# SwiGLU gate and up products streamed in two halves of 256 columns

## The chip, the cores and the metric

The kernel runs on one NeuronCore of a Trainium2 chip. The metric is the device time of one execution in microseconds (us). Three runs of the kernel before took 2365.91, 2370.27 and 2372.9 us; their median is 2370.27.

## The reference

A decoder trunk of two layers over 512 positions with a model width of 1024. Each layer computes a half-step of a gated feed-forward network (FFN), a mixer of three kinds of attention heads, a second FFN half-step, and a gated per-layer embedding. The part that the change touches is the FFN, with an inner width of 2816; it occurs twice in each layer, four times in all:

```python
def swiglu(h, w_gate, w_up, w_down):
    return (jax.nn.silu(h @ w_gate) * (h @ w_up)) @ w_down

for i in range(DEPTH):                       # DEPTH = 2
    x = x + 0.5 * swiglu(rms_norm(x, ffn1_norm[i]), ffn1_w_gate[i], ffn1_w_up[i], ffn1_w_down[i])
    x = x + hybrid_mixer(rms_norm(x, mix_norm[i]), ...)
    x = x + 0.5 * swiglu(rms_norm(x, ffn2_norm[i]), ffn2_w_gate[i], ffn2_w_up[i], ffn2_w_down[i])
    ...
```

All inputs are float32. `h @ w_gate` is 512 x 1024 by 1024 x 2816.

## The kernel before

**Layout.** The residual stream x is kept transposed in on-chip memory: 8 tiles of 128 features by 512 positions (KT = 8, P = 128, SEQ = 512). A product puts a weight block of 128 x 128 into TensorE as the stationary operand and streams the 512 positions of one tile of x past it, so an output is 128 output features by 512 positions in one bank of the accumulation memory (2 KB per partition, 512 float32). The norm is applied afterwards: a product is scaled by a factor per position (tile rb).

**Precision.** Every weight and every activation is split in two float32r parts, a rounded one and the rest (wh and wl, xh and xl). A product of one block is three matmuls, made by `three` (lines 502 to 505): wh with xh, wh with xl, and wl with xh, all accumulated in the same bank. Line 503 is the first, 504 the second, 505 the third. Each matmul of the language makes two records in the profile, a weight load (PEld, LDWEIGHTS) and a matmul (PE, MATMUL).

**FFN on TensorE.** `ffn` (line 541) runs over FT = 22 tiles of the inner width. For each tile `ft` it makes the gate product and then the up product with `from_x` (line 512): it takes the next of four banks, waits until the chunk's split weights are there, runs over the 8 blocks k with three matmuls each, 24 in all, and lets the last matmul increase the semaphore "product". The gate product of `ft` 0 waits before each block for the x tile that it needs; in the second FFN it takes the blocks in another order. After the up product of `ft` 0 comes the sum of squares for the norm (`sum_squares`, line 531). After all 22 tiles the down products follow (ffh and ffl are the streamed operands there).

**The other engines in an FFN.** The weights come in chunks of 512 KB, one per product, into three slots of raw, wh and wl. SyncE's queue (line 430) issues a chunk's transfer when the split of the chunk three before is complete. ScalarE rounds raw to wh (line 955) once the product that used the slot is done; VectorE subtracts to get wl (line 1425). For each tile VectorE scales the gate product (line 1512) when its "product" semaphore has come, ScalarE takes the SiLU (line 1019), VectorE scales the up product (line 1525), multiplies (line 1530) and subtracts (line 1518), and ScalarE rounds the result to ffh (line 1024). The order on each engine is written out by hand; engines meet only at semaphores.

**Other stages that the prediction reads.** In the mixer's group C four chunks of "natural" products stream 402 columns of weights past blocks of xh and xl, with the same `three`. `compressed_scores` (line 759) makes products of 128-column weights with 64 streamed columns in plain float32, `transposes` (line 801) turns 128 x 128 blocks.

Of the kernel before, what the change touches and what calls it, by code (L numbers as in the profile page):

```python
# [41 lines left out]
P = 128  # L42
D_MODEL, SEQ, DEPTH, PLE_DIM, D_FF = 1024, 512, 2, 256, 2816
# [11 lines left out]
KT = D_MODEL // P  # L55
# [115 lines left out]
def chunk_width(key):  # L171
    if key[0].startswith("nat"):
        return 2 * NAT[key[0][3]]
    if key[0].endswith("_down"):
        a, b = THIRDS[key[2]]
        return (b - a) * P
    if key[0] == "wout_early":
        return len(LOADED) * P
    if key[0] == "wout_late":
        return 2 * len(LATE) * P  # L180
    return WIDE
# [15 lines left out]
class Counts:  # L197
# [13 lines left out]
    def tick(self, kind, *key, frees=None, layer=None):  # L211

        key = (self.layer if layer is None else layer, *key)
        self.n[kind] = self.n.get(kind, 0) + 1
        assert (kind, *key) not in self.seen, (kind, *key)
        self.seen[(kind, *key)] = self.n[kind]
        if frees is not None:
            content = (self.layer, frees)
            assert content not in self.frees, content
            self.frees[content] = (kind, *key)  # L220
        return self.sem(kind), 1

    def done(self, kind, *key, layer=None):

        if not self.known:
            return self.sem(kind), 1
        return self.sem(kind), self.known["seen"][(kind, self.layer if layer is None else layer, *key)]

    def freed(self, content, layer=None):

        if not self.known:
            return self.sem("any"), 1
        kind, layer, *key = self.known["frees"][(self.layer if layer is None else layer, content)]
        return self.done(kind, *key, layer=layer)
# [6 lines left out]
def layers(nc, a, known):  # L241
# [3 lines left out]
    with ctx:  # L245
# [6 lines left out]
        def sb(name, shape, dt=F32):  # L252
            size = int(np.prod(shape[1:])) * 4
            t = nc.alloc_sbuf_tensor_at(name, shape, dt, offset=place["at"])
            place["at"] += (size + 63) // 64 * 64
            assert place["at"] <= 229344, (name, place["at"])
            return t

        x = sb("x_res", [P, KT, SEQ])
        xh, xl = sb("xh", [P, KT, SEQ], F32R), sb("xl", [P, KT, SEQ], F32R)  # L260
# [121 lines left out]
        tick, done, freed = counts.tick, counts.done, counts.freed  # L382
# [26 lines left out]
        with nc.Block() as block:  # L409
# [74 lines left out]
            def _(pe):  # L484
                turn, held = {0: 0, 1: 0, 2: 0}, {}

                def take(content, which=1, at=None):

                    if which == 2:
                        which, at = SHARED[turn[2] % len(SHARED)]  # L490
                        turn[2] += 1
                    elif at is None:
                        at = turn[which] % 4
                        turn[which] += 1
                    if (which, at) in held:
                        layer, old = held[which, at]
                        pe.wait_ge(*freed(old, layer=layer))
                    held[which, at] = (counts.layer, content)
                    counts.bank[(counts.layer, content)] = (which, at)
                    return (main, side)[which][at]  # L500

                def three(out, lh, ll, rh, rl, start, stop, **kw):
                    nc.tensor.matmul(out, lh, rh, start=start, stop=False, **kw)  # L503
                    nc.tensor.matmul(out, lh, rl, start=False, stop=False, **kw)  # L504
                    return nc.tensor.matmul(out, ll, rh, start=False, stop=stop, **kw)  # L505

                def chunk(key):
                    c, n = counts.layer * NCHUNKS + CHUNK[key], chunk_width(key)
                    pe.wait_ge(*done("weights_lo", c, layer="all"))
                    return wh[:, c % SLOTS, 0:n], wl[:, c % SLOTS, 0:n]  # L510

                def from_x(key, stage=None, at=None, order=tuple(range(KT)), read=False):

                    out = take(key, 0, at)
                    h, l = chunk(key)
                    for k in order:
                        if stage:
                            pe.wait_ge(*done("x_lo", stage, k))
                        ks = slice(k * P, (k + 1) * P)
                        mm = three(out[:], h[:, ks], l[:, ks], xh[:, k, :], xl[:, k, :], k == order[0],  # L520
                                   k == order[-1])
                        if read and k < KT - 1:
                            mm.then_inc(*tick("x_read", k))
                    mm.then_inc(*tick("product", key))

                def sum_squares(name):

                    out = take(("squares", name))
                    pe.wait_ge(const_in, 16)
                    pe.wait_ge(*done("squares_added", name, KT - 1))  # L530
                    nc.tensor.matmul(out[:], const_("ones"), acc[:], start=True,
                                     stop=True).then_inc(*tick("squares", name))

                def head_squares(name, blocks, n=SEQ, which=1):
# [3 lines left out]
                    nc.tensor.matmul(out[:, 0:n], const_(blocks), zs[:, slot_of(name) % 2, 0:n], start=True,  # L538
                                     stop=True).then_inc(*tick("head_squares", name))

                def ffn(name):
                    for ft in range(FT):
                        if ft:
                            from_x((name + "_gate", ft))
                        else:
                            from_x((name + "_gate", ft), name,
                                   order=EARLY + LATE if name == "ffn2" else tuple(range(KT)))
                        from_x((name + "_up", ft))
                        if ft == 0:
                            sum_squares(name)  # L550
                    for dt in range(KT):
                        out = take((name + "_down", dt), 0)
                        for third, (lo, hi) in enumerate(THIRDS):
                            key = (name + "_down", dt, third)
                            h, l = chunk(key)
                            for f in range(lo, hi):
                                if dt == 0:
                                    pe.wait_ge(*done("h_lo", name, f))
                                fs = slice((f - lo) * P, (f - lo + 1) * P)
                                mm = three(out[:], h[:, fs], l[:, fs], ffh[:, f, :], ffl[:, f, :], f == 0,  # L560
                                           f == FT - 1)
                            if third < 2:
                                mm.then_inc(*tick("product", key))

                        mm.then_inc(*tick("product", key))
# [343 lines left out]
                for layer in range(DEPTH):  # L909
                    counts.layer = layer  # L910
                    ffn("ffn1")
                    group_c()
                    hgrn()
                    attention()
                    products_out()
                    ffn("ffn2")
                    for h2 in range(2):
                        key = ("ple_proj", h2)
                        h, l = chunk(key)
                        pe.wait_ge(*done("emb_lo", 1))  # L920
                        for d in range(4):
                            out = take(("ple_out", 4 * h2 + d), 0)
                            for k in range(2):
                                ks = slice((2 * d + k) * P, (2 * d + k + 1) * P)
                                mm = three(out[:], h[:, ks], l[:, ks], embh[:, k, :], embl[:, k, :], k == 0, k == 1)
                            mm.then_inc(*(tick("product", key) if d == 3 else tick("product", key, d)))
                        if h2 == 0:
                            sum_squares("ple")
                    for dt in range(KT):
                        from_x(("ple_gate", dt), "ple" if dt == 0 else None, read=dt == KT - 1 and layer < DEPTH - 1)  # L930
                        if dt == 0:
                            sum_squares("post")
# [1210 lines left out]
```

## Time and profile before

| | |
|---|---|
| median of 3 runs | 2370.27 us |
| profiled execution | 2371.97 us |
| its span (first to last instruction) | 2370.2 us |
| mean granted TensorE clock | 0.984 |
| instructions recorded | 27606 |
| TensorE matmul busy | 2286.1 us, 96%, 10816 matmuls |
| TensorE weight load busy | 1803.5 us, 76%, 10816 loads |
| VectorE busy | 1208.1 us, 51% |
| ScalarE busy | 901.6 us, 38% |

Busy time is the time in which at least one instruction of that kind is in flight. Matmuls are pipelined: one starts before the one ahead has left the array, so the duration of a single matmul is longer than the step from one start to the next, and the step is what a row of matmuls costs. Weight loads run beside matmuls and have rows of their own. The granted clock is given as a share of 2.4 GHz.

### The profile page before, as it was taken

To read this page: it belongs to the slowest core of one execution; us is meant where nothing else is said; L and a number is where in the kernel's file an instruction comes from. 1 tells how busy PE (TensorE), PEld (TensorE's weight loads), DVE (VectorE), ACT (ScalarE), POOL (GpSimd) and SP (SyncE) were. 2 spreads that over 40 slices of the span, in tenths; PEclk is the share of its full clock that TensorE was granted. 3 is DMA by queue.
4 is the path that set the end of the run, shared out by engine and by line. 5 is a ranking of instruction groups with operands and counts; after the bars stand their busy time and mean duration, and the time that the engine had idled before them with its cause. 6 is when DMAs were issued, how large, how long until landed. Compare 5 with 4: busy or idle time off the path is not lost. (4 is left out here: it accounts for less than half of the span.)

```text
span 2370.2 us, 27606 instructions
## 1 busy us (share of the span) xinstructions
PE 2286.1 (96%) x10816; PEld 1803.5 (76%) x10816; DVE 1208.1 (51%) x1990; ACT 901.6 (38%) x1483; POOL 82.6 (3%) x119
## 2 busy tenths in 40 slices
PE   8999999899989999999999999998989889999998
PEld 6888887776656788888778888877766568888887
DVE  5444334465676444433564443345657764444335
ACT  5222223444654323222453232244445643232224
POOL 0000000032000000000000000001310000000000
PEclk9999999999989999999999999999999899999999
DMA  5333334211102233333233333343121023333332
GB/s 193 121 98 98 91 96 150 94 54 63 45 21 78 89 98 93 99 99 102 89 98 90 98 95 98 99 132 102 55 72 34 21 80 98 98 95 99 98 101 80
DMA packets 68986, 214.31 MB, mean 90 GB/s; under 512 B 8143, under 2 KB 15311, under 8 KB 68858
## 3 DMA queue, kind: packets, MB, share of 16 engines
q1 hardware_dynamic: 59344, 189.27, 26.2%
q10 hardware_dynamic: 9514, 23.27, 2.9%
q8 instruction: 87, 1.43, 0.2%
q14 instruction: 41, 0.34, 0.0%
HBM read 208.30 MB, written 5.40 MB: 90 GB/s over the span
## 5 line engine op out<-in xcount | busy, mean ns | idle before, releaser
L503 PE MATMUL main<-xh,wh 128*128 128x512 f32 x1944 | 778.0, 400 | 16.4 <-DVE xl L1432 12.5
L504 PE MATMUL main<-xl,wh 128*128 128x512 f32 x1944 | 761.9, 392 | 0.0
L505 PE MATMUL main<-xh,wl 128*128 128x512 f32 x1944 | 761.5, 392 | 0.0
L1425 DVE TENSOR_TENSOR wl<-raw,wh 128x1024 fp32r<-128x1024 f32 (+3 forms) x372 | 440.1, 1184 | 399.9 <-ACT wh L955 399.0
L955 ACT ACTIVATE wh<-raw 128x1024 fp32r<-128x1024 f32 (+3 forms) x372 | 378.2, 1017 | 498.2 <-PE main L505 466.6
L503 PEld LDWEIGHTS main<-xh,wh 128*128 128x128 f32 x1944 | 367.6, 189 | 121.8 <-issue 21.2
L505 PEld LDWEIGHTS main<-xh,wl 128*128 128x128 f32 x1944 | 367.9, 189 | 78.1
L504 PEld LDWEIGHTS main<-xl,wh 128*128 128x128 f32 x1944 | 368.0, 189 | 77.9 <-issue 4.3
L503 PE MATMUL main<-ffh,wh 128*128 128x512 f32 x704 | 273.9, 389 | 0.0
L504 PE MATMUL main<-ffl,wh 128*128 128x512 f32 x704 | 273.9, 389 | 0.0
L505 PE MATMUL main<-ffh,wl 128*128 128x512 f32 x704 | 273.9, 389 | 0.0
L1019 ACT ACTIVATE fg<-fg 128x512 f32<-128x512 f32 x88 | 55.7, 632 | 403.6 <-DVE fg L1512 403.5
L1512 DVE TENSOR_TENSOR fg<-main,rb 128x512 f32<-128x512 f32 x88 | 60.8, 691 | 240.0 <-PE main L505 225.2
L504 PEld LDWEIGHTS main<-ffl,wh 128*128 128x128 f32 x704 | 132.2, 188 | 27.5
L505 PEld LDWEIGHTS main<-ffh,wl 128*128 128x128 f32 x704 | 132.2, 188 | 27.4
L503 PEld LDWEIGHTS main<-ffh,wh 128*128 128x128 f32 x704 | 132.2, 188 | 27.4
L1525 DVE TENSOR_TENSOR fu<-main,rb 128x512 f32<-128x512 f32 x88 | 60.8, 691 | 156.4 <-PE main L505 156.4
L1300 ACT ACTIVATE probs<-probs,small 128x128 f32<-128x128 f32 (+3 forms) x160 | 87.7, 551 | 38.5 <-DVE small L1827 38.5
L476 POOL TENSOR_TENSOR zv<-ev,hall 128x256 f32<-128x256 f32 x108 | 80.4, 767 | 317.0 <-ACT ev L1117 218.4
L1668 DVE COPY_PREDICATED sdiag<-lmask,side 128x512 f32<-128x512 uint32 x84 | 57.1, 733 | 42.5 <-PE side L621 42.5
L621 PEld LDWEIGHTS side<-zv 64*128 64x128 f32 x768 | 48.1, 187 | 29.1 <-issue 24.7
L621 PE MATMUL side<-zv 64*128 64x128 f32 (+1 forms) x768 | 59.4, 292 | 8.0 <-DVE cp L1788 5.2
(230 smaller groups left out, 1937.7 us busy)
## 6 DMA issues: line engine op xcount, KB each, us to landing
raw<-in_ffn_gate SPq DMA_DIRECT2D x88, 512.0 KB, 3.6
raw<-in_ffn_up SPq DMA_DIRECT2D x88, 512.0 KB, 3.6
raw<-in_ffn_down SPq DMA_DIRECT2D x64, 448.0 KB, 3.3
raw<-in_w_in_t SPq DMA_DIRECT2D x40, 512.0 KB, 3.6
raw<-in_ffn_down SPq DMA_DIRECT2D x32, 512.0 KB, 3.5
raw<-in_wout SPq DMA_DIRECT2D x24, 384.0 KB, 3.1
w<-in_cmp_w ACTq DMA_DIRECT2D x16, 512.0 KB, 3.6
raw<-in_ple_gate SPq DMA_DIRECT2D x16, 512.0 KB, 3.2
```

Of the source, the lines that this page charges most:

```text
L476: nc.gpsimd.tensor_tensor(o.rearrange(cut, two=2, l=size)[:, :, which, :], e.rearrange(cut, two=2, l=size)[:, :, which, :], operand.rearra ...
L503: nc.tensor.matmul(out, lh, rh, start=start, stop=False, **kw)
L504: nc.tensor.matmul(out, lh, rl, start=False, stop=False, **kw)
L505: return nc.tensor.matmul(out, ll, rh, start=False, stop=stop, **kw)
L621: mm = nc.tensor.matmul(outs[hh][:, o:o + w], first[:, s:s + P], second[:, t:t + w], start=True, stop=True)
L955: nc.scalar.activation(wh[:, c % SLOTS, 0:n], raw[:, c % SLOTS, 0:n], ACT.Copy).then_inc(*tick("weights_hi", c, layer="all"))
L1019: nc.scalar.activation(fg[:, ft % 2, :], fg[:, ft % 2, :], ACT.Silu).then_inc(*tick("gate_silu", name, ft))
L1300: nc.scalar.activation(pr, pr, ACT.Exp, bias=sm("nm", k), scale=-1.0, accum_out=sm("sum", k)).then_inc(*tick("probs", u, g, i))
L1425: nc.vector.tensor_tensor(wl[:, c % SLOTS, 0:n], raw[:, c % SLOTS, 0:n], wh[:, c % SLOTS, 0:n], ALU.subtract).then_inc(*tick("weights_lo", ...
L1512: nc.vector.tensor_tensor(fg[:, ft % 2, :], bank_of((name + "_gate", ft))[:], rb[:], ALU.mult).then_inc(*tick("gate_scaled", name, ft, fre ...
L1525: nc.vector.tensor_tensor(fu[:, ft % 2, :], bank_of((name + "_up", ft))[:], rb[:], ALU.mult).then_inc(*tick("up_scaled", name, ft, frees=( ...
L1668: ins = V.copy_predicated(out, m, src)
```

## The change

A function `in_halves` stands beside `from_x`. For each weight block it runs `three` twice, over positions 0 to 255 and over 256 to 511, into the two halves of the same bank: six matmuls of 256 columns for three of 512. Only the very first matmul of a product has the start flag; both halves of the last block end with the stop flag. The last matmul of all increases the same semaphore as before. `ffn` calls it for every up product and for all gate products but that of `ft` 0. Nothing changes on other engines, in the down products, in the mixer or in the embedding.

```diff
+                def in_halves(key, stage=None):
+
+                    out = take(key, 0)
+                    h, l = chunk(key)
+                    for k in range(KT):
+                        if stage:
+                            pe.wait_ge(*done("x_lo", stage, k))
+                        ks = slice(k * P, (k + 1) * P)
+                        for half in range(2):
+                            ns = slice(half * SEQ // 2, (half + 1) * SEQ // 2)
+                            mm = three(out[:, ns], h[:, ks], l[:, ks], xh[:, k, ns], xl[:, k, ns], k + half == 0,
+                                       k == KT - 1, skip_group_check=True)
+                    mm.then_inc(*tick("product", key))
+
                 def ffn(name):
                     for ft in range(FT):
                         if ft:
-                            from_x((name + "_gate", ft))
+                            in_halves((name + "_gate", ft))
                         else:
                             from_x((name + "_gate", ft), name,
                                    order=EARLY + LATE if name == "ffn2" else tuple(range(KT)))
-                        from_x((name + "_up", ft))
+                        in_halves((name + "_up", ft))
                         if ft == 0:
                             sum_squares(name)
```

## Rows read from the trace of the kernel before

**Rows 1.** Profile page: span, busy time by engine, granted clock in 40 slices.
```profile
span 2370.2 us, 27606 instructions
...
PE 2286.1 (96%) x10816; PEld 1803.5 (76%) x10816; DVE 1208.1 (51%) x1990; ACT 901.6 (38%) x1483; POOL 82.6 (3%) x119
...
PEclk9999999999989999999999999999999899999999
```

**Rows 2.** Windows, FFN stretches: length, busy and count by engine, PEclk, DMA share, GB/s.
```profile
28.00:256.00 228.00, 228.00 (x1007) 188.69 (x1005) 108.30 (x147) 73.60 (x93) 0.00 (x0) 1.00 0.35 111
...
785.00:1012.00 227.00, 227.00 (x1003) 187.94 (x1002) 105.68 (x126) 68.96 (x88) 0.00 (x0) 1.00 0.31 95
1205.00:1434.00 229.00, 229.00 (x1010) 189.26 (x1009) 108.93 (x148) 74.26 (x94) 0.00 (x0) 1.00 0.32 96
1961.00:2187.00 226.00, 226.00 (x999) 187.20 (x998) 104.89 (x125) 67.23 (x86) 0.00 (x0) 1.00 0.31 96
```

**Rows 3.** Groups of instructions, 28.7 to 256 us: count | busy, mean ns | idle before.
```profile
L503 PE MATMUL main<-xh,wh 128*128 128x512 f32 x335 | 130.3, 389 | 0.0
L503 PEld LDWEIGHTS main<-xh,wh 128*128 128x128 f32 x335 | 62.9, 188 | 13.1
...
L955 ACT ACTIVATE wh<-raw 128x1024 fp32r<-128x1024 f32 x41 | 43.1, 1052 | 50.3 <-PE main L505 50.3
L1512 DVE TENSOR_TENSOR fg<-main,rb 128x512 f32<-128x512 f32 x22 | 15.2, 691 | 56.7 <-PE main L505 54.9 <-ACT rb L982 1.9
```

**Rows 4.** Timeline inside gate and up products: start us, duration us, engine, instruction.
```profile
100.28 0.39 PE L503 MATMUL main<-xh,wh 128*128 128x512 f32 x1
100.28 0.19 PEld L504 LDWEIGHTS main<-xl,wh 128*128 128x128 f32 x1
...
103.68 0.39 PE L503 MATMUL main<-xh,wh 128*128 128x512 f32 x1
...
109.12 0.39 PE L503 MATMUL main<-xh,wh 128*128 128x512 f32 x1
```

**Rows 5.** Timeline at the start, the granted clock still at 1.2 GHz.
```profile
16.29 0.63 PE L503 MATMUL main<-xh,wh 128*128 128x512 f32 x1
...
18.42 0.63 PE L505 MATMUL main<-xh,wl 128*128 128x512 f32 x1
```

**Rows 6.** Timeline of the natural products of group C, 402 columns.
```profile
444.18 0.34 PE L505 MATMUL main<-wh,xl 128*128 128x402 f32 x1
...
446.02 0.34 PE L503 MATMUL main<-wh,xh 128*128 128x402 f32 x1
...
444.19 0.19 PEld L503 LDWEIGHTS main<-wh,xh 128*128 128x128 f32 x1
```

**Rows 7.** Timeline of a restart of TensorE at 584.6 us.
```profile
584.61 0.19 PEld L503 LDWEIGHTS main<-xh,wh 128*128 128x128 f32 x1 [0.33 <-issue]
584.61 0.50 PE L503 MATMUL main<-xh,wh 128*128 128x512 f32 x1
...
584.72 0.19 PEld L504 LDWEIGHTS main<-xl,wh 128*128 128x128 f32 x1
```

**Rows 8.** Timeline of dense runs: 24 score products, 11 transposes (merged rows).
```profile
556.09 2.88 PEld L759 LDWEIGHTS side<-kc,q 128*128 128x128 f32 x24
556.32 2.79 PE L759 MATMUL side<-kc,q 128*128 128x64 f32 x24
...
649.42 1.35 PEld L801 LDWEIGHTS side<-const,probs 128*128 128x128 f32 x11
649.65 1.36 PE L801 MATMUL side<-const,probs 128*128 128x128 f32 x11
```

**Rows 9.** Timeline: the two square-sum products in plain float32; one lasts 0.59 us.
```profile
27.29 1.02 PE L531 MATMUL side<-acc,const 128*128 128x512 f32 x2
...
L531 PE MATMUL side<-acc,const x20: 590/590/591, 27.3 to 2326.1; 128*128 128x512 f32 x20
```

**Rows 10.** DMA queues of the page: packets, MB, share of 16 engines' time.
```profile
q8 instruction: 87, 1.43, 0.2%
```

## Prediction, made before the changed kernel was run

> **What bounds the kernel now.** I began with the page. TensorE's matmul row is busy for 2286.1 of 2370.2 us, against 51% for VectorE and 38% for ScalarE, and the granted clock is 9 tenths or more in nearly every slice [rows 1]. Busy time of pipelined matmuls does not say what one costs, so I then read the four stretches in which the changed products run, 910 us in all: matmul is busy in every microsecond of them, at a granted clock of 1.00 (2.4 GHz) [rows 2]. In the groups of instructions of the first stretch the matmuls have 0.0 us of idle before them, while VectorE and ScalarE sit idle waiting for a product (54.9 us in 22 scalings of a gate product, 50.3 us in 41 splits of weights) [rows 3]. So in these stretches TensorE sets the pace and every nanosecond of the start-to-start step of its matmuls is on the path. The timeline gives that step: 24 matmuls between 103.68 and 109.12 us, 5.44 us / 24 = 226.7 ns [rows 4]. The duration shown for one (389 ns) is its latency, and no price for the sum.
>
> **What changes in number.** A gate or up product is now 8 weight blocks x 3 matmuls of 512 columns = 24. Each becomes 48 of 256 columns. The first gate product of each of the four FFN calls keeps its form, so 4 x (21 + 22) = 172 products change: 4128 matmuls and 4128 weight loads go, 8256 of each come. Today every matmul has its own load, also where the next one uses the same weights (as many load as matmul records, 335 and 335 for the same line) [rows 3], so the second half loads all three blocks again. Nothing is saved for that: the columns streamed are the same. With P for the step at 256 columns, the change costs 4128 x (2P - 226.7 ns). It pays off only below P = 113.3 ns.
>
> **What P can be, from below.** Streaming 256 columns at 2.4 GHz takes 106.7 ns. A load also needs time of its own. At a restart the second load starts 0.11 us after the first and the first matmul, recorded as 0.50 us where 0.39 is usual, really starts then too [rows 7]: a load of 128 columns takes some 107 to 110 ns before its matmul can go on. Where the streaming is much shorter than that, the load is the step: the 24 score products with 64 moving columns have 24 loads in 2.88 us; without the last one's duration (0.19) and the longer first gap (0.23), 2.46 / 22 = 111.8 ns [rows 8]. Transposes of 128 columns with 128-column loads go every (1.36 - 0.27) / 10 = 109 ns [rows 8]. So loads hide up to a step of about 112 ns and P is not below 111.8. That end of the range is a gain of 4128 x 3.1 ns = 13 us, with the load in front instead of the stream.
>
> **What P can be, from above.** At 512 columns the step is 226.7 where the columns alone are 213.3: 13.4 ns too many. At the 1.2 GHz level the surplus is gone: 5 matmuls in 2.13 us are 426 ns, the 512 columns alone 426.7 [rows 5]. The question of this change is what the 13.4 ns belong to. If to the columns (6.3% more for each), 256 columns take 113.3 and the change is free. If to the matmul with its load, 256 columns take 106.7 + 13.4 = 120.0, and 4128 x 13.3 = 55 us are added. The one other width of this number format in the trace is 402 columns: 10 steps in 1.84 us, 184.0 ns, 16.5 over its 167.5 [rows 6]. By the proportional reading it should be 178, by the fixed one 180.9; it is above both and nearer the fixed one. Its rows of 402 x 4 bytes start off a power of two, which may cost a little that halves of 256 don't pay. A surplus of 16.5 would give 123.2 and +81 us; a straight line through both widths (0.388 ns a column) 127.3 and +115 us. I take 120.0, as the 512-column row has the tensor and alignment of the changed code.
>
> A rule of the Trainium skill bears on this. The surplus at 2.4 GHz measured above is 13.4 ns; the skill (TensorE: Matmul & The Clock Gate, Back-to-back issue gap) states a gap of N/2.4 + 2.5 ns, for an isolated matmul and not named for this number format. The 4-byte products of the square sums, two 512-column ones in 1.02 us, step by 1.02 - 0.59 = 0.43 us [rows 9], close to twice 213.3, so a small surplus as in that rule does occur in this kernel, but the row of the changed products doesn't follow it. By that rule the change would cost 4128 x 2.5 ns = 10 us.
>
> **What else the edit touches.** The semaphore increment stays on the last matmul of a product, and the wait for weights ahead of the first, so VectorE, ScalarE and the weight queue see the same events, each product at most some 0.3 us later (24 x 13.3 ns). They wait for TensorE today [rows 3], so none of this is late. Cover for nothing is removed: the weight chunks are read in the same order, and a slower product gives their transfer and splits more time. The bank is started once, by the first half of the first block, and costs no instruction. Instruction fetch: 1.43 MB in 87 packets, 0.2% of the DMA engines [rows 10], is 66 bytes for each of the 21632 matmul and load records if it is all theirs. Two records every 120 ns would be 1.1 GB/s beside the 95 to 111 GB/s of these stretches [rows 2]; I cost it at nothing. If it couldn't keep up, TensorE would wait for instructions, which no row of the old kernel excludes at 8256 pairs on end; the longest dense run is about 24 [rows 8]. The clock stays up in either case, since TensorE never rests.
>
> **Sum.** Profiled execution 2371.97 us (span 2370.2 and 1.8 around it) + 55 = 2427; the median of the runs shown is 1.7 lower, so 2425.3, said as 2426.
>
> **Rivals.**
> 1. The surplus belongs to the columns (P 111.8 to 114.5): -13 to +10 us, 2357 to 2380. For it: a read rate that a 2.4 GHz stream just exceeds would give a surplus for each column and none at 1.2 GHz, as [rows 5] have it, and the surplus per matmul of [rows 9] is small. Against: the 184 ns of [rows 6], which this reading puts at 178. This is the case that ends on the other side: if a 256-column stream and a load fit under each other with less loss than a 512-column one, steps below 113.3 make the kernel faster. It decides below 113.3 ns, and the load-bound 111.8 caps the gain at 13 us. Chance 25%: 4 faster by over 0.3% (7.1 us), 15 within, 6 slower (P above 114.2).
> 2. The forecast, P 117 to 124: +30 to +88 us. Chance 45%.
> 3. Loads and streams share something: (512 + 128) / 226.7 = 2.82 columns per ns and (402 + 128) / 184.0 = 2.88 agree within 2%. Then (256 + 128) / 2.85 = 134.7 and +176 us, 2546; with the straight line above this case runs from P 125 to 136. Against it: each half of the agreement rests on one width, and the 402-column rows already carry an alignment of their own. Chance 20%.
> 4. A load must end before the next matmul starts: its record is 188 ns [rows 3], it starts with the matmul before it [rows 4], so P = 188 and 4128 x 149.3 = +616 us, 2986; or instruction supply binds somewhere between. Against: at 402 columns the next matmul starts every 184 ns, before the load's record ends [rows 6], and the dense run with 0.19 us loads goes every 112 ns [rows 8]. Chance 10%, most of it for something smaller than 188.
>    Loads are busy 62.9 x 3 = 189 of 228 us in the first stretch, 83% [rows 2, 3]. By the Trainium skill (Perfetto Trace Analysis, Identifying the Most-Contended Engine) it is the load's busy share, not the matmul's, that tells the headroom; twice the loads would be 166% and it speaks for this rival. But busy loads overlap in [rows 8] (24 x 0.19 us in 2.88 us), so I don't take that share as a bound.
> 5. The change does not do what it says, for instance a second load dropped where weights repeat: today none is dropped, so it is inside the above and has no chance of its own.
>
> **Numbers.** About 0.3% (7.1 us) is what a measurement of this kernel can tell from no change. Faster 4%; same 15%; slower 45 + 6 + 20 + 10 = 81%. The likeliest case's own range is 2400 to 2458. For 8 in 10 I reach down to 2368 (P at 113) and up to 2500 (P at 129), leaving out the gain (3), the upper part of rival 3 (7) and rival 4 (10).
>
> **What the new profile would show.** 14944 matmul and load records in place of 10816; in the gate stretches groups of 128x256 with 2752 records a line (8256 / 3) beside 512-column groups; a product of 48 matmuls taking 48P: 5.44 us if free, 5.76 by my forecast, 6.5 by rival 3, 9.0 by rival 4. The down products' step should stay 226.7 and the rest of the kernel unchanged, granted clock 1.00 in the gate stretches. If loads start evenly spaced and well after the matmul before them, the load is the bound; if they start with it, the stream is. I am wrong in direction if 48 matmuls take less than 5.42 us, and wrong in kind if the extra time stands as idle time ahead of matmuls (engine or instruction waits) and not in their steps.

## The result, and the profile after

The changed kernel takes 2425.76 us (median of 4 runs, 2417.94 to 2427.51), the kernel before 2368.09 on the same chip. The ratio is 1.0237, 95% interval 1.0205 to 1.0268: slower by 2.4%. The forecast was 2426.

The page of the kernel after, to be read against [rows 1]: 8256 records more, 4128 of them matmuls and 4128 loads. TensorE is as busy as before in share of the span and 51.9 us busier; the load row, which is where the doubled loads show, has grown by 213 us. VectorE and ScalarE have the same work.

```profile
span 2423.5 us, 35862 instructions
...
PE 2338.0 (96%) x14944; PEld 2016.7 (83%) x14944; DVE 1208.3 (50%) x1990; ACT 902.4 (37%) x1483; POOL 82.7 (3%) x119
...
PEclk9999999999999999999999999999999899999999
```

The groups of instructions of the first changed stretch (28.7 to 267 us), against [rows 3]. No idle time stands before a matmul; the engines behind it wait longer than before (62.4 us in place of 56.7 ahead of the scaling of the gate products, 56.6 in place of 50.3 ahead of the splits).

```profile
L503 PE MATMUL main<-xh,wh 128*128 128x256 f32 x663 | 187.6, 283 | 0.0
L503 PEld LDWEIGHTS main<-xh,wh 128*128 128x128 f32 x662 | 127.1, 192 | 0.0
...
L969 ACT ACTIVATE wh<-raw 128x1024 fp32r<-128x1024 f32 x41 | 43.2, 1054 | 56.6 <-PE main L505 56.6
L1526 DVE TENSOR_TENSOR fg<-main,rb 128x512 f32<-128x512 f32 x22 | 15.2, 691 | 62.4 <-PE main L505 60.9 <-ACT rb L996 1.5
```

The window of that stretch, against [rows 2]: matmul and load busy throughout, granted clock 1.00.

```profile
28.00:267.00 239.00, 239.00 (x1992) 238.81 (x1991) 107.86 (x148) 73.87 (x94) 0.00 (x0) 1.00 0.34 107
```

The timeline inside the new products, against [rows 4]: a load starts with the matmul ahead of it (both at 100.06 us), and 48 matmuls go from 100.18 to 105.94 us, 5.76 us / 48 = 120.0 ns. Over all 8248 neighbouring pairs of 256 columns the mean without the gaps is 120.00.

```profile
100.06 0.28 PE L505 MATMUL main<-xh,wl 128*128 128x256 f32 x1
100.06 0.19 PEld L503 LDWEIGHTS main<-xh,wh 128*128 128x128 f32 x1
...
100.18 0.28 PE L503 MATMUL main<-xh,wh 128*128 128x256 f32 x1
...
105.94 0.28 PE L503 MATMUL main<-xh,wh 128*128 128x256 f32 x1
```

Where the time went, by stage. The marks are the starts of TensorE's square sums and of the first down product in the traces; us. A gate/up stretch here begins behind the two products of tile 0, so it holds 42 changed products. "Mixer" is everything between the down products of FFN 1 and the square sums of FFN 2.

```
stage            before: layer 0, layer 1    after: layer 0, layer 1
gate/up, FFN 1          229.4   229.4            242.8   242.8
gate/up, FFN 2          229.4   229.4            242.8   242.8
down, each              125.1   125.1            125.1   125.1
mixer                   401.7   398.0            397.6   401.4
```

The first stretch ends with the first down product, at 256.68 us in the kernel before and 270.10 us in the changed one:

```profile
256.68 0.39 PE L503 MATMUL main<-ffh,wh 128*128 128x512 f32 x1
```

```profile
27.30 0.63 PE L531 MATMUL side<-acc,const 128*128 128x512 f32 x1
...
270.10 0.40 PE L503 MATMUL main<-ffh,wh 128*128 128x512 f32 x1
```

Each of the four stretches grew by 13.4 us: 42 x 24 x 13.3 ns. With the four up products of tile 0 that makes 55, and the span grew by 53.3. The rest is the mixer and the start, which move by some us from execution to execution, and so does the time that the granted clock spends at 1.2 GHz. By the profile's record of that clock, which begins 18 to 19 us after the first instruction, it is 74 us before and 67 after.

### The profile page after: what moved, and what is told of

It reads as the page before. It is cut to its first block and busy times, and to the rows that moved or that the text cites. A ratio compares the mean times of both kernels' runs of the same rounds, so it can differ in the third digit from the quotient of the medians.

```text
span 2423.5 us, 35862 instructions
## 1 busy us (share of the span) xinstructions
PE 2338.0 (96%) x14944; PEld 2016.7 (83%) x14944; DVE 1208.3 (50%) x1990; ACT 902.4 (37%) x1483; POOL 82.7 (3%) x119
## 5 line engine op out<-in xcount | busy, mean ns | idle before, releaser
L503 PE MATMUL main<-xh,wh 128*128 128x256 f32 (+1 forms) x3320 | 1021.7, 308 | 16.2 <-DVE xl L1446 12.4
L504 PE MATMUL main<-xl,wh 128*128 128x256 f32 (+1 forms) x3320 | 1005.0, 303 | 0.0
L505 PE MATMUL main<-xh,wl 128*128 128x256 f32 (+1 forms) x3320 | 1005.0, 303 | 0.0
L503 PEld LDWEIGHTS main<-xh,wh 128*128 128x128 f32 x3320 | 630.7, 190 | 67.9 <-issue 21.9
L504 PEld LDWEIGHTS main<-xl,wh 128*128 128x128 f32 x3320 | 631.2, 190 | 24.3 <-issue 4.3
L505 PEld LDWEIGHTS main<-xh,wl 128*128 128x128 f32 x3320 | 630.7, 190 | 24.3
```

## The experiments

The theory of the prediction: a step is the streamed columns at 2.4 GHz plus 13.3 ns, but no less than the 111.8 ns that a 128-column load needs. The rivals are a cost of the stretch as a whole, a cost of the order, and a surplus that hangs on something other than the matmul count. Experiments 3 to 8 ask what the surplus hangs on.

**1. Half of the change.** Only the up products in halves.

```diff
                         if ft:
-                            in_halves((name + "_gate", ft))
+                            from_x((name + "_gate", ft))
```

> Only the up products run in halves, the gate products go back to 512 columns. Theory (each matmul pays a fixed 13.3 ns on top of its columns, whatever its width): 88 products x 24 matmuls x 13.3 ns = 28.2 us over the kernel before, half of the change's 55; step 120.0 ns in the up products, 226.7 in the gate products, ratio 1.012. Rival (the cost is one of the stretch as a whole, such as instruction supply or the weight slots running late): gate products alone give the other engines and the fetch time to catch up, and the cost is well under half.

2397.17 us against 2368.61, ratio 1.0119 (1.0101 to 1.0136): +28.6 us for 28.2. Each of the four stretches takes 236.5 us, within 0.4 us of halfway between 229.4 and 242.8. The cost adds up matmul by matmul; nothing in it points to the other engines or to the supply of instructions, and experiment 8 settles that supply, since there the same number of instructions takes 113.3 ns each.

**2. Another order, twice.** First the halves as the outer loop.

```diff
-                    for k in range(KT):
-                        ks = slice(k * P, (k + 1) * P)
-                        for half in range(2):
-                            ns = slice(half * SEQ // 2, (half + 1) * SEQ // 2)
+                    for half in range(2):
+                        ns = slice(half * SEQ // 2, (half + 1) * SEQ // 2)
+                        for k in range(KT):
+                            ks = slice(k * P, (k + 1) * P)
```

> The loop over the two halves is outside the one over the weight blocks: all 24 matmuls on columns 0 to 255, then 24 on 256 to 511, same number and size. Theory (fixed cost per matmul): step 120.0 ns and the same time as the changed kernel, 2424 to 2427 us. Rival (returning to the same weight block or hopping between the halves of the bank costs or saves something): another step, by more than 1 ns, that is over 8 us in all.

2421.84 us. The four stretches take 242.8 us as in the changed kernel, mean step 119.99 ns; the 4 us less, which also put the time 2 us under the expected range, lie outside them, in an execution with 50 us recorded at the low clock in place of 67. Then equal weights side by side:

```diff
+                        for n, (weights, moving) in enumerate(((h, xh), (h, xl), (l, xh))):
+                            for half in range(2):
+                                ns = slice(half * SEQ // 2, (half + 1) * SEQ // 2)
+                                mm = nc.tensor.matmul(out[:, ns], weights[:, ks], moving[:, k, ns],
...
```

> Halves with the order turned so that equal weights stand next to each other: both halves of wh with xh, both of wh with xl, both of wl with xh; four loads of wh follow each other. Theory (every matmul loads its weights again, whatever was there): 14944 loads, step 120.0 ns, the time of the changed kernel, 2420 to 2427 us. Rival (a repeated load is cheaper or is skipped): fewer load records or a step towards the 113.3 ns at which the change would be free, about 2370 us.

2431.07 us (before: 2371.2 beside it), 4 us over the expected range, with 81 us recorded at the low clock; 14944 loads, mean step 120.00 ns, stretches 242.8 us again. A repeated load is made all the same, and the step does not change. So neither of two other orders rescues the change. Whether a repeated load is a cheaper one can't be seen here, as the step is longer than a load needs.

**3. Narrower pieces: is there a load floor?**

```diff
-                        for half in range(2):
-                            ns = slice(half * SEQ // 2, (half + 1) * SEQ // 2)
+                        for n, (lo, hi) in enumerate(((0, 128), (128, 256), (256, 384), (384, 512))):
+                            ns = slice(lo, hi)
...
```

> The same products cut into four pieces of 128 columns, with four loads a block. Theory with a load floor: the stream would need 66.7 ns, but each 128-column load holds the next matmul until 111.8 ns, so 4 x 111.8 = 447 ns in place of 226.7, 4128 x 220.5 = +910 us, about 3280 us, loads evenly spaced at 112 ns and no longer starting with a matmul. Rival, only the fixed cost of a matmul counts: 4 x 66.7 = 266.7, +165 us, about 2535 us.

3278.12 us, 2 us from the forecast of the floor. Its timeline shows how a load-bound stretch looks: the loads come every 112 ns, in between the matmuls' starts, where in the stream-bound one they start with a matmul. 24 matmuls from 149.86 to 152.54 us are 111.7 ns each. It is one execution, as are those of experiments 4 to 7; they are read by their steps.

```profile
149.86 0.27 PE L503 MATMUL main<-xh,wh 128*128 128x128 f32 x1
149.91 0.19 PEld L504 LDWEIGHTS main<-xl,wh 128*128 128x128 f32 x1
149.97 0.28 PE L504 MATMUL main<-xl,wh 128*128 128x128 f32 x1
150.02 0.19 PEld L505 LDWEIGHTS main<-xh,wl 128*128 128x128 f32 x1
...
152.54 0.27 PE L503 MATMUL main<-xh,wh 128*128 128x128 f32 x1
```

**4. Uneven pieces.** The same edit with `((0, 384), (384, 512))`:

> The same products cut unevenly, 384 + 128 columns. Theory (step = the larger of columns / 2.4 GHz + 13.3 ns and the 111.8 ns that a 128-column load needs): 173.3 for the wide piece, about 112 for the narrow one, pair 285.3 ns in place of 226.7, 4128 x 58.6 = +242 us, about 2610 us. Rival without a load floor: 173.3 + 66.7 = 240.0, the same +55 us as the halves, 2424 us.

2619.91 us: 10 above the forecast, far from the rival's 2424. A block of six takes 150.34 to 151.20 us, 0.863 by all of them where 0.856 was expected. If the three narrow ones take 111.7 each, 176 ns are left for a wide one, 2.6 more than 173.3. And with `((0, 402), (402, 512))`:

> Cut 402 + 110 columns, the wide piece starting at the beginning of its row. It asks what lay behind the 184.0 ns of the 402-column products of the mixer. If their rows, which start off a power of two, were the cause: 167.5 + 13.3 = 180.8 ns here. If 402 columns cost more by their number: 184.0. If the surplus is a share of the columns: 178.0. The 110-column piece is under the load floor: 112 ns in each case. Pair 290 to 296 ns, +261 to +286 us, 2630 to 2655 us.

2656.05 us, 1 above the expected range; the steps inside the 402-column group are 183.3 and 180.8 on average. Starting a row evenly takes only 1 to 3 of the 184.0 ns away. Both runs say that 13.3 ns is not one price for all widths. One more thing stands in this trace: three of its four stretches take 296.5 or 296.6 us, a mean step of 146.67 ns, and FFN 2 of layer 0 takes 299.9 us at 148.33, with the same instructions.

```profile
150.34 0.40 PE L503 MATMUL main<-xh,wh 128*128 128x384 f32 x1
150.57 0.34 PE L504 MATMUL main<-xl,wh 128*128 128x384 f32 x1
150.75 0.34 PE L505 MATMUL main<-xh,wl 128*128 128x384 f32 x1
150.92 0.22 PE L503 MATMUL main<-xh,wh 128*128 128x128 f32 x1
150.98 0.27 PE L504 MATMUL main<-xl,wh 128*128 128x128 f32 x1
151.09 0.28 PE L505 MATMUL main<-xh,wl 128*128 128x128 f32 x1
151.20 0.39 PE L503 MATMUL main<-xh,wh 128*128 128x384 f32 x1
```

**5. Fewer weight columns: what does the surplus hang on?**

```diff
+                    m = 64 if key[1] >= 4 else P
                     for k in range(KT):
...
-                        ks = slice(k * P, (k + 1) * P)
...
+                        ks = slice(k * P, k * P + m)
+                        for n, (lo, hi) in enumerate(((0, 512),)):
...
-                            mm = three(out[:, ns], ...
+                            mm = three(out[0:m, ns], ...
```

The first two runs stream 512 columns in one piece again, the third one four pieces of 128; in each the first four tiles of an FFN keep all 128 weight columns.

> One matmul of 512 columns per block again, but from the fifth tile of each FFN on only 64 of the 128 weight columns are loaded (left out: half the output features of 144 of the 172 products, the bank's other rows keep what was there). It asks what the surplus of 13.3 ns hangs on. If on the loaded columns (the load takes a share of the stream's time, 0.104 ns a column): half, 6.7 ns, step 220.0, 3456 x 6.7 = 23 us under the kernel before, about 2346 us. If it is one of the matmul, whatever is loaded: step 226.7 and the time of the kernel before, 2369 us.

> As the run with 64 weight columns, with 32 (left out: three quarters of the output features of the same 144 products). If the surplus hangs on the loaded columns: 3.3 ns, step 216.7, 35 us under the kernel before, about 2334 us. If it belongs to the matmul: 226.7 again, 2369 us.

Both expectations missed, on the same side. 2381.58 us with 64 weight columns and 2384.13 with 32, against 2367.19, one execution each: a smaller load makes the 512-column matmul slower. 12 steps take 2.76 us in the timeline, 230 ns; with 32 columns the mean is 231.7. The surplus is neither a share of the load nor fixed.

```profile
149.72 0.40 PE L503 MATMUL main<-xh,wh 128*64 128x512 f32 x1
...
152.48 0.40 PE L503 MATMUL main<-xh,wh 128*64 128x512 f32 x1
```

> Four pieces of 128 columns, with 64 weight columns loaded from the fifth tile of each FFN on (left out: half the output features there). The other 28 products are quarters with full loads, 672 x 220.5 = +148 us. For the 144: a load of 64 columns should hold a matmul for about 58 ns only (53 + 4.5), so the stream binds again. Surplus on loaded columns: 53.3 + 6.7 = 60.0 ns, 3456 x (240 - 226.7) = +46, about 2563 us. Surplus of the matmul: 66.7 ns, +138, about 2655 us. If the load floor doesn't shrink with the loaded columns: 111.8 here too, +762, about 3280 us.

2560.37 us, 60.0 ns a step (24 in 1.44 us), 3 us from the forecast for a surplus on the loaded columns. The two runs before had already refuted that one, so its match is no support. What stays is that the floor shrinks with the loaded columns, and that the surplus at 128 streamed columns is 6.7 ns, half of 13.3.

```profile
150.49 0.22 PE L503 MATMUL main<-xh,wh 128*64 128x128 f32 x1
...
151.93 0.22 PE L503 MATMUL main<-xh,wh 128*64 128x128 f32 x1
```

**6. A table of widths.** One kernel in which each tile's products stream one shape over and over.

```diff
+                    if key[1] >= 4:
+                        m, n, at = (GATES if key[0].endswith("gate") else UPS)[key[1] - 4]
                     for k in range(KT):
-                        ks = slice(k * P, (k + 1) * P)
-                        for half in range(2):
-                            ns = slice(half * SEQ // 2, (half + 1) * SEQ // 2)
+                        ks = slice(k * P, k * P + m)
+                        for rep in range(-(-SEQ // n)):
+                            ns = slice(at, at + n)
...
```

> A table of steps in one run. From the fifth tile of each FFN on, each gate product streams one width over and over into the first columns of its bank, as often as it takes to reach 512 columns in all, with 128 weight columns: 128, 160, 192, 224, 240, 256, 272, 288, 320, 352, 384, 402, 416, 432, 448, 480, 496, 512 streamed columns. The up products do so with 64, 32 and 96 weight columns, and with 256 columns that start at 8, 64 and 256 (left out: all columns and features outside these, and columns are added more than once, so the outputs are not the model's). The total time says nothing here, the steps do. Theory 1 (fixed cost of a matmul, 13.3 ns, under a load floor of 111.8): 111.8 up to 224 columns (224 gives 106.7), then columns / 2.4 + 13.3: 113.3 at 240, 120.0 at 256, 146.7 at 320, 180.8 at 402, 200.0 at 448, 226.7 at 512, the same at every start. Theory 2 (after the runs with 64 weight columns, 60.0 ns at 128 columns and 230 at 512): a surplus of about 3.3 ns + 0.026 ns a column, which with 64 weight columns gives 116.7 at 256 and 173.3 at 384, and with 128 weight columns breaks down only because something adds a few ns to the narrow ones. Theory 3: the surplus comes in whole steps, least where the width divides evenly into 256, 13.3 ns there and 15 to 17 in between, as 402 and 384 showed.

The steps, worked out from the starts of each product of 24 to 96 matmuls without its first two, median of four products of a shape; the four agree within 0.04 ns (for 128 weight and 512 streamed columns the step of the unchanged products). In brackets what stands above columns / 2.4 GHz.

```
streamed columns    128 weight columns    96              64             32
128                 111.7  (load floor)   85.0            60.0  (6.7)    60.0  (6.7)
160                 111.7  (load floor)
192                 111.6  (load floor)                   88.7  (8.7)
224                 111.7  (load floor)
240                 112.0
256                 120.0  (13.3)         116.0 (9.3)     113.5 (6.8)    113.3 (6.7)
272                 125.2  (11.9)
288                 131.7  (11.7)
320                 146.6  (13.3)                         144.4 (11.1)
352                 160.0  (13.3)
384                 173.3  (13.3)                         173.3 (13.3)   173.2 (13.2)
402                 183.5  (16.0)
416                 188.2  (14.9)
432                 196.1  (16.1)
448                 202.7  (16.0)                         202.4 (15.8)
480                 216.7  (16.7)
496                 223.3  (16.7)
512                 226.7  (13.3)         229.9 (16.6)    230.1 (16.7)   231.1 (17.8)
```

With 128 weight columns, 256 streamed ones that start at column 64 step by 119.8 ns, at 256 by 120.0, and 384 that start at 128 by 173.9.

None of the three theories holds as written. Theory 1 has the floor up to 224 and, with full loads, the value at 256, 320, 352, 384 and 512, but not at 240 (112.0, not 113.3), at 272 and 288, nor from 402 to 496. Theory 2 misses at 256 with 64 weight columns (113.5, not 116.7), theory 3 at 320, 272 and 288. What the narrow loads show is a surplus near 6.7 ns at 128 and 256 columns and near 13.3 at 384. Against that, 256 columns beside a full load pay 6.7 ns extra, and one entry hints why: started at column 8, the same 256 columns stepped by 116.8 ns.

**7. A table of places.** The same kernel form with width, place in the bank, start in xh and start of the weights as the varied quantities.

```diff
-                            mm = three(out[0:m, ns], h[:, ks], l[:, ks], xh[:, k, ns], xl[:, k, ns], ...
+                            mm = three(out[:, to:to + n], h[:, ks], l[:, ks], xh[:, k, at:at + n],
+                                       xl[:, k, at:at + n], ...
```

> A second table of steps: does the place of the operands set the surplus? In the first table 256 columns that start at column 8 stepped by 116.8 ns, those that start at 0 or 256 by 120.0. From the fifth tile of each FFN on the gate products stream 256 columns, and 480, that start at 0, 2, 4, 8, 12, 16, 20 or 24, 32, 64 in xh and xl, into the first columns of the bank; up products write 256 or 480 columns from 4, 8, 16 or 32 on in the bank; others read 256 or 512 columns with the 128 weight columns taken from 4, 8, 16, 32, 64 or 96 on; one has all three shifted by 8 or 0. The eighth weight block is left out (the shifted weights would run past the chunk), and columns are added more than once, so the outputs are not the model's. Theory A (where the streamed row starts against where the weights start decides, two reads of the same memory meet): the step changes with the start in xh (116.8 at 8) and with the start of the weights, not with the place in the bank. Theory B (where the output starts in the bank decides): it changes with that alone. Theory C (the 116.8 needed both): neither alone. If a shift of the weights takes the 512-column step below 226.7 ns, a kernel with that layout is faster than both; 1 ns on the 10816 matmuls is 11 us.

```
                         256 columns                        512 columns         480 columns
all at 0                 120.0                              226.7               216.6
place in the bank        120.0 at 4 and 8, 119.6 at 16,                         216.9 at 8, 16
                         119.9 at 32                                            and 32
start in xh and xl       120.0 at 2, 118.7 at 4, 117.8                          214.6 at 2, 216.8 at 4,
                         at 8, 118.3 at 12, 117.8 at 16,                        217.8 at 12, 218.3 at
                         119.8 at 24, 118.7 at 32,                              16, 217.6 at 20, 220.0
                         119.9 at 64                                            at 8, 24 and 32
start of the weights     118.4 at 4, 118.2 at 8,            233.3 at 4, 8, 16
                         113.4 at 16, 120.1 at 64           and 96; 232.7 at
                                                            32; 228.4 at 64
weights and xh both at 8 119.9
```

Theory A: the place in the bank moves the step by 0.4 ns at most, the place of weights against stream by up to 6.7, and shifting both alike gives the old value back. Weights from column 16 on take the step of 256 columns to the 113.4 at which the change would be free, and that of 512 columns up to 233.3. Of the seven places tried the layout of the kernel before has the best one for 512. That two reads of the same memory meet, as theory A puts it, is a guess at the reason that no run tests. Nor do width and start fix a step to the last ns: 256 columns from column 8 stepped by 116.8 ns in the first table and by 117.8 in this one, which leaves the eighth weight block out. What else differs between the two is open.

```profile
168.04 0.28 PE L503 MATMUL main<-xh,wh 128*128 128x256 f32 x1
...
170.76 0.28 PE L503 MATMUL main<-xh,wh 128*128 128x256 f32 x1
```

```profile
223.78 0.39 PE L503 MATMUL main<-xh,wh 128*128 128x512 f32 x1
...
226.58 0.39 PE L503 MATMUL main<-xh,wh 128*128 128x512 f32 x1
```

(Weights from column 16 on: 24 steps of 256 columns in 2.72 us, 12 of 512 columns in 2.80 us.)

**8. The changed kernel with the weights 64 bytes further on.**

```diff
+        place["at"] += 64
         wh, wl = sb("wh", [P, SLOTS, WIDE], F32R), sb("wl", [P, SLOTS, WIDE], F32R)
...
-        place["at"] = region + (P - region) % 2048
+        place["at"] = region + (P + 64 - region) % 2048
         ffh, ffl = sb("ffh", [P, FT, SEQ], F32R), sb("ffl", [P, FT, SEQ], F32R)
```

Everything placed behind wl moves by the same 64 bytes.

> The changed kernel with one edit of layout and none of the work: wh and wl lie 64 bytes (16 columns) further on against xh and xl; ffh and ffl move with them, so that the down products keep their alignment. Theory (13.3 ns at 256 columns is 6.7 ns that go with 256 streamed columns and 6.7 ns of the weight read and the stream meeting in memory; the table had 113.36 ns for weights from column 16 on): gate and up products step by 113.4 ns instead of 120.0, 8256 x 6.6 = -55 us; the products of 512 columns out of xh, some 1824 matmuls, go from 226.7 to 233.3, +12 us; down products stay at 226.7. Together 43 us under the changed kernel, about 2383 us, ratio to the kernel before 1.006. Rival (13.3 ns are a fixed price of a matmul with its load, as the prediction had it, and 113.36 came from the single table entry's own conditions, such as the same block over and over): step 120.0 and 2426 us or more.

2374.3 us against 2367.37, ratio 1.0027 (1.0013 to 1.004), 9 us below the expectation: with the same 14944 matmuls and loads, seven eighths of the change's cost is gone. Three of the four stretches take 229.4, 229.3 and 229.3 us, those of the kernel before. The timeline has 48 steps in 5.44 us, 113.3 ns:

```profile
99.94 0.28 PE L504 MATMUL main<-xh,wh 128*128 128x256 f32 x1
...
105.38 0.28 PE L504 MATMUL main<-xh,wh 128*128 128x256 f32 x1
```

The 512-column products out of xh step by 233.3 ns, as forecast. The remaining stretch, FFN 1 of layer 1, takes 238.4 us, and it does so evenly, 117.8 ns from end to end (48 steps from 1300.06 to 1305.71 us in 5.65 us):

```profile
1300.06 0.28 PE L504 MATMUL main<-xh,wh 128*128 128x256 f32 x1
...
1305.71 0.28 PE L504 MATMUL main<-xh,wh 128*128 128x256 f32 x1
```

So this layout has two paces, and this stretch kept one of them from end to end, as the one of 299.9 us in experiment 4 did. One stretch at the slow pace is 9 us, which is also the distance between the lowest and the highest group of its runs (2370.5 to 2371.3 and 2380.1 to 2381.2; four lie at 2373.4 to 2375.0). Only one of these runs, one of the highest group, has a profile, so that the lowest group has no slow stretch is likely and not shown, and what picks the pace is open. In the layout of the change no second pace was seen: all 16 stretches of the four profiled executions with 256 columns (the changed kernel, experiments 1 and 2) step by 120.0 ns there.

The total can be estimated from the profiled executions. The changed kernel's span is 2423.5 us; the stretches and the up products of tile 0 give back 46. The 512-column products out of xh cost some 8 more and not 12, because with their restarts they stepped by 228.2 ns on average outside the stretches, not by 226.7. The recorded time at the low clock is 55 us and not 67, worth some 6 where TensorE sets the pace. That makes 2380, and the span is 2378.3.

The expectation overlooked what this layout would do to the kernel before. With 233.3 ns for one matmul of 512 columns and 113.3 for each of 256, two halves take 226.7 ns and are the shorter way, by 4128 x 6.7 ns = 27 us as an estimate from these steps. The kernel before with moved weights was not run, so this stays an estimate; but by the steps measured the sign of the change depends on the layout.

## Why the prediction was right, and where its reason was not

- **TensorE sets the pace, each nanosecond of step is on the path.** Right: no idle time ahead of a matmul, 53.6 us of growth in the four stretches where the span grew by 53.3, and half the change costs half.
- **4128 x (2P - 226.7).** Right in count and form: 14944 records of each kind, 2752 matmuls a line, 13.4 us for each stretch.
- **P = 120.0.** Right to 0.1 ns, also that the 402-column row was the worse guide. The bounds held too: 111.8 from the score products came back as 111.7 in the quarters, and the load's record of 188 ns was no bound.
- **The reason given for 120.0**, that the 13.4 ns at 512 columns are a price of the matmul with its load and come again in full at 256, was wrong as a general statement and right only as a number in this layout. With weights 64 bytes further on, 256 columns cost 113.3, and narrow loads give the same. So at 256 columns 6.7 of the 13.3 ns go with the place of the weights against the stream. No row of the kernel before could separate this: its 512-column products shared one alignment, and the 402-column rows differed in width and alignment at once. That 6.7 + 6.7 at 256 columns equals the 13.3 that 512 columns pay at the best place tried was luck, as far as these runs tell. In the moved layout the same forecast would have been off by most of the effect: 55 us forecast, 7 measured. Why the place matters, and why the surplus at 512 columns is 13.3 ns, stays open.
- **Rival 1, the surplus goes with the columns.** Its number, 113.3, came true in the moved layout, its mechanism did not. There 512 columns pay 20.0 ns where 256 pay 6.7, and with 64 weight columns 128 streamed columns pay 6.7 and 256 pay 6.8. The surplus does not grow in proportion.
- **Rival 3, a shared capacity of 2.85 columns per ns.** Refuted: 120.0 where it wanted 134.7, and fewer loaded columns made 512 columns slower, not faster. Load and stream are not independent, though: the step depends on their place and on the number of loaded columns. With fewer of them it falls at 256 streamed columns (120.0, 116.0, 113.5, 113.3 ns with 128, 96, 64, 32) and rises at 512.
- **Rival 4, and the busy share of loads.** Refuted. Loads are busy for 238.8 of the 239 us of the changed stretch and the step is still the stream's; the load bound begins at 111.7 ns. So the headroom by the load row, which the Trainium skill asks for (Perfetto Trace Analysis, Identifying the Most-Contended Engine), warned of the right side but not at the right point: with the load row busy throughout, the matmuls still stepped by 120.0 ns, 8.3 above the load bound. The supply of instructions does not bind either: with 64 weight columns in quarters a load and a matmul went by every 60.0 ns.
- **The rule of the Trainium skill for the gap**, N/2.4 + 2.5 ns (TensorE: Matmul & The Clock Gate, Back-to-back issue gap): the products of this number format never came to it. Their least surplus in the tables is 6.7 ns.

## What to carry to other kernels

In a stretch that TensorE bounds, cutting a product into narrower matmuls streams no column less, and each additional one costs what it pays above its columns; read that from the step between starts in the timeline, never from durations or busy shares. A matmul whose columns take less time than its weight load (here 111.7 ns for 128 columns, so below about 240 streamed columns) is bound by the load. One width in a trace can't tell a fixed price from a proportional one, and two widths can't either: at one alignment the surplus went between 11.7 and 16.7 ns from 256 to 512 columns, up and down. Before trusting such a split, measure the width in question, and when the width of a matmul changes, try the place of weights against stream again.

## What the runs showed of the hardware that was not expected

- The relative place of stationary and streamed operand changes the step of float32r matmuls by up to 6.7 ns: 113.4 to 120.1 ns at 256 columns, 226.7 to 233.3 at 512, and the best place tried for 256 (weights from column 16) is among the worst for 512.
- Loading fewer weight columns makes a 512-column matmul slower: 226.7 ns with 128, 229.9 with 96, 230.1 with 64, 231.1 to 231.7 with 32.
- A stretch of equal matmuls can run at one of two paces, 113.3 or 117.8 ns, and stay there for 229 us or more; seen in the moved layout and, with 146.67 and 148.33 ns, in the cut 402 + 110.
- Matmuls of 128 to 240 columns beside a 128-column load all cost 111.6 to 112.0 ns; with 96 weight columns 128 streamed ones cost 85.0 ns, and with 64 the floor is at or below 60.
